# A ring of six value pages where the spread queries lay: paged attention in a two-layer decoder step

## The reference, cut to what matters

```python
def fox_sample(q, k, v, logf, k_pool, v_pool, lf_pool, page_table):
    k_past = k_pool[page_table].reshape(bd, p_len, h, d)
    v_past = v_pool[page_table].reshape(bd, p_len, h, d)
    ...
    s_past = (jnp.einsum('bqhd,bkhd->bhqk', q, k_past).astype(jnp.float32) * scale
              + cq[..., :, None] + jnp.transpose(r_past, (0, 2, 1))[:, :, None, :])
    ...
    p = jax.nn.softmax(jnp.concatenate([s_past, s_new], axis=-1), axis=-1)
    return (jnp.einsum('bhqk,bkhd->bqhd', p[..., :p_len].astype(v.dtype), v_past)
            + jnp.einsum('bhqk,bkhd->bqhd', p[..., p_len:].astype(v.dtype), v))
```

## Time and profile before

| | |
|---|---|
| median of 3 runs | 2034.9 us (2031.11 to 2038.15) |
| the profiled execution | 2039.11 us, span 2037.5 us |
| TensorE busy, weight loads busy | 87%, 75% of the span |
| VectorE, ScalarE, GpSimd busy | 47%, 27%, 5% |
| DMA over the span | 110 GB/s; in the loop over slots 230 to 270 GB/s |
| mean granted TensorE clock | 0.925 |

### The profile page before, as it was taken

The page is one execution under the profiler, slowest core; times in us unless marked ns, Lnnn a source line. Parts: engine busy times, 40 slices in busy tenths (PEclk is TensorE's granted clock), DMA queues, the critical chain, the costliest instruction groups (busy, mean ns, idle before and its releaser), DMA issues.

```text
span 2037.5 us, 37876 instructions
## 1 busy us (share of the span) xinstructions
PE 1767.3 (87%) x15111; PEld 1537.3 (75%) x15111; DVE 948.9 (47%) x1377; ACT 556.1 (27%) x992; POOL 105.1 (5%) x208
## 2 busy tenths in 40 slices
PE   5999555989999999799966787777779899999998
PEld 4876433979999999799944444444439799999997
DVE  5388776453333322467455755555513533333222
ACT  3210223232222211243331333333312322222110
POOL 1000000000000000144410000000000000000000
PEclk9999876999999999999977788888879899999999
DMA  3211031222222323222341677777662122223221
GB/s 117 61 43 32 24 96 42 83 62 81 80 81 80 95 72 85 66 71 76 102 164 58 218 260 256 262 264 271 239 197 77 55 82 82 82 82 98 72 85 60
DMA packets 239470, 224.79 MB, mean 110 GB/s; under 512 B 12114, under 2 KB 199588, under 8 KB 239354
## 3 DMA queue, kind: packets, MB, share of 16 engines
q1 hardware_dynamic: 229168, 200.83, 31.7%
q0 software_dynamic: 8768, 19.09, 2.9%
q10 hardware_dynamic: 1418, 3.29, 0.5%
HBM read 215.37 MB, written 7.80 MB: 110 GB/s over the span
## 4 chain that ended last, share of the span: by engine, by line
PE 74%; DVE 12%; DMA 5%; issue 3%; ACT 3%; SPq 3%; ACTq 0%; DVEq 0%; POOL 0%; POOLq 0%
PE ps L1484 56%; DMA vring<-in_cache_fox_v_dram 4%; PE ps L1897 4%; PE ps L1673 3%; PE ps L1942 2%; PE ps L1466 1%; DVE tmp L438 1%; SPq L2060 1%; PE ps L1876 1%; DVE yc L717 1%; DVE aL L442 1%; DVE rb L448 1%; DVE rb L433 1%; PE ps L1535 1%; PE ps L1858 1%
## 5 line engine op out<-in xcount | busy, mean ns | idle before, releaser
L1484 PE MATMUL ps<-aH,wH 128*128 128x288 f32 x2224 | 488.3, 301 | 49.8 <-DVE aL L442 34.2
L1484 PE MATMUL ps<-aL,wH 128*128 128x288 f32 x2224 | 480.7, 298 | 0.0
L1484 PE MATMUL ps<-aH,wL 128*128 128x288 f32 x2224 | 480.4, 298 | 0.0
L1484 PEld LDWEIGHTS ps<-aH,wH 128*128 128x128 f32 x2224 | 362.2, 191 | 59.3 <-issue 35.6
L419 DVE TENSOR_TENSOR wL<-raw,wH 128x1024 fp32r<-128x1024 f32 (+1 forms) x179 | 232.0, 1296 | 338.4 <-ACT wH L1053 335.3
L1484 PEld LDWEIGHTS ps<-aL,wH 128*128 128x128 f32 x2224 | 363.1, 191 | 0.0
L1484 PEld LDWEIGHTS ps<-aH,wL 128*128 128x128 f32 x2224 | 362.5, 191 | 0.0
L1053 ACT ACTIVATE wH<-raw 128x1024 fp32r<-128x1024 f32 (+1 forms) x179 | 199.0, 1112 | 388.0 <-PE ps L1484 359.4
L1484 PE MATMUL ps<-gH,wH 128*128 128x288 f32 x704 | 151.8, 297 | 4.8 <-DVE gL L635 4.8
L1484 PE MATMUL ps<-gL,wH 128*128 128x288 f32 x704 | 151.5, 296 | 0.0
L1484 PE MATMUL ps<-gH,wL 128*128 128x288 f32 x704 | 151.5, 296 | 0.0
(11 more groups left out here) (306 smaller groups left out, 1788.3 us busy)
## 6 DMA issues: line engine op xcount, KB each, us to landing
kset<-in_cache_fox_k_dram SPq DMA_DIRECT2D x128, 384.0 KB, 4.2
vring<-in_cache_fox_v_dram SPq DMA_DIRECT2D x128, 384.0 KB, 4.8
raw<-in_w_gate_up_dram SPq DMA_DIRECT2D x88, 512.0 KB, 3.7
raw<-in_w_down_dram SPq DMA_DIRECT2D x32, 704.0 KB, 4.6
raw<-in_fox_w_in_dram SPq DMA_DIRECT2D x21, 512.0 KB, 4.0
raw<-in_w_out_dram SPq DMA_DIRECT2D x16, 512.0 KB, 3.9
raw<-in_conv_w_in_dram SPq DMA_DIRECT2D x14, 512.0 KB, 3.9
raw<-in_w_mem_kv_dram SPq DMA_DIRECT2D x8, 512.0 KB, 3.7
```

Of the source, the lines that this page charges most:

```text
L1484: mm = nc.tensor.matmul(ps[:, 2 * slot + h, 0:HT], weights[:, w], a[:, k0 + k, h * HT:(h + 1) * HT], start=(first and k == 0 and weights i ...
```

## The change

The value ring gets six buffers in place of four. The two new ones take the bytes of `qr`, which is removed with its 16 copies, its semaphore and ACT's two waits ahead of them. `spread` instead copies each sequence's queries straight from `qkT` into `qx4`, with 16 instructions of 32 partitions x 48 elements where there were four of 128 x 48. The SP queue keeps its order of keys and values; at each place where a value page was issued, the page two further on is issued, and it waits for the same page to be used as before (page n now waits for page n-6, not n-4). Six pages, not four, are issued ahead of the turns. SP's loop gets one more turn, in which nothing is issued. TensorE's and VectorE's instructions stay as they are.

```diff
-    VRING = 4
+    VRING = 6
...
-        qr, o = at("qr", [P, NH, 2, NS], o)
...
-            act.wait_ge(hn_done, Z + 1 + HP)
-            act.wait_ge(mL_done, KD)
-            for e in range(2):
-                for c in range(2):
-                    r = slice(DH * e + DQ * c, DH * e + DQ * c + DQ)
-                    for a in range(4):
-                        last = nc.scalar.activation(qr[DQ * a:DQ * a + DQ].rearrange("p (g e) c n -> p g e c n", e=2)[:, :, e, c, :],
-                                                    qkT[r, 0:HP, SEQ:T], ACT.Copy)
-            last.then_inc(qr_done, 1)
...
-                for m in range(4):
-                    nc.scalar.activation(qx4[:].rearrange("p (j m c) n -> p j m c n", m=4, c=2)[:, :, m, :, NQ * m:NQ * m + NQ],
-                                         qr[:].rearrange("p (j m) c n -> p j m c n", m=4)[:, :, m, :, NQ * b:NQ * b + NQ], ACT.Copy)
+                for e in range(2):
+                    for c in range(2):
+                        for a in range(4):
+                            rows = slice(DH * e + DQ * c, DH * e + DQ * c + DQ)
+                            mine = qx4[DQ * a:DQ * a + DQ, 2 * e + c, NQ * e:NQ * e + NQ]
+                            mine = bass.AP(tensor=mine.tensor, offset=mine.offset, ap=[mine.ap[0], [8 * QR, 3], [4 * QR + 2 * NQ, 2], [1, NQ]])
+                            nc.scalar.activation(mine, qkT[rows, 0:HP, SEQ + NQ * b:SEQ + NQ * b + NQ].rearrange("p (j m) q -> p j m q", m=2), ACT.Copy)
...
-            for s in range(SLOTS + SPB - 1):
+            for s in range(SLOTS + SPB):
...
-                for n in range(4 * (s - 3), 4 * (s - 2)):
-                    if n >= VRING:
+                for n in range(4 * (s - 4) + VRING, 4 * (s - 3) + VRING):
+                    if VRING <= n < NB * NP:
                         value_page(n)
```

More of the change, by code:

```diff
@@ L352, in build @@
         e_done, zab_done, c_ready, c_done, stage_done = (sem(n) for n in ("e_done", "zab_done", "c_ready", "c_done", "stage_done"))
-        lftot_done, qr_done, clear_done = (sem(n) for n in ("lftot_done", "qr_done", "clear_done"))
+        lftot_done, clear_done = (sem(n) for n in ("lftot_done", "clear_done"))
         turn_ready = sem("turn_ready")
```

## The result

The change made the kernel slower by 0.4%: 2046.16 us as a median of 9 runs (2042.56 to 2053.17), beside 2037.78 us (2030.58 to 2041.2) for the kernel before on the same chip; ratio 1.0044, 95% interval 1.003 to 1.0059. The profiled execution took 2050.02 us, span 2048.4; the mean granted clock of TensorE went from 0.925 to 0.917. The forecast was 2005 us, faster.

The account below looks back on a forecast made before the run. Weight products, untouched, were 56% of the span's chain; in the slot loop, value-page landings held TensorE. Odd slots 35 plus drain 9.5 less spread 15 made 30 us less: 2005 us on the median, range 1991 to 2026.

Parts of the forecast that it names:

- The ring's mechanism: Twelve odd slots, 5 to 27: the batch's first landing gates the third page, no longer the first; wait 46.9 to about 20.
- The first landing: T0, when an odd slot's first value page issued behind the keys lands, some 9 us behind the set; taken to stay.
- The burst's 4 us: Page bursts follow each other without rest, so landings come later: 0 to 13 us over twelve slots, 4 taken as cost.
- the fetch: TensorE's 2.27 us stop in second sets, read as code fetch behind page traffic, grows: 0 to 22 us, 6 taken.
- The ring's sum: Odd slots gain 45.4 us, less 4 for the burst and 6 for code fetch: 35 us; the drain adds 9.5.
- The working of slot 13: Slot 13: values ahead of the landing run at their shorter durations, so the next set begins 3.96 us earlier.
- The drain: From slot 28 on, values alone: the last sixteen pages' issues take 16.7 us instead of 26.06, 9.5 us less.
- The spread: ACT's query copies ahead of first sets: twelve more cost 1.9 us a spread, 15 us over eight (12 to 23).
- `qr`: Its sixteen building copies on ACT, 0.52 us each, end; 7.9 us of slack there, so nothing gained.
- The slower one: Rival: moving between quadrants sets the copy's price, 7.8 us more a spread, 62 in all: 2052 us; chance 0.08.
- The copies that do not overlap: Rival: short spread copies at 0.34 us each, 39 us more in all: 2029 us, about no change; chance 0.05.
- The wait that only moves: Rival: TensorE can't run the step's values ahead of the landing, a slot gains some 1.5 us: 2026 to 2039; chance 0.07.

Follow-up runs that it names:

- the ring alone: The changed kernel with six value buffers but the spread as four wide copies without the quadrant shift (wrong queries): 2011.69 us, ratio 0.989 to the kernel before.
- the spread alone: The changed kernel with its sixteen narrow spread copies and no `qr`, but four value buffers in the old load order: 2072.48 us, ratio 1.0181 to the kernel before.
- the moved reduction: The changed kernel with the sample's first reduction on VectorE moved from the fourth slot's head to the third's end: 2037.52 us, ratio 1.0016 to the kernel before.
- the run without the shift between quadrants: The changed kernel with its sixteen spread copies reading the same quadrant that they write (wrong queries): 2041.08 us.
- the queue's run on the kernel before: The kernel before with SP's queue alternating two key pages and two value pages in each turn, nothing else: 2048.88 us, ratio 1.0079.
- the queue interleaved: The changed kernel with spread copies on GpSimd, early sample reduction, and SP's queue alternating two key and two value pages: 1998.77 us, ratio 0.9817 to the kernel before.

## Why the prediction was wrong

- **The ring's mechanism: right.** The wait stands at the third page, 1.42 us in the row above, and ahead of the drain it is 17.7 us in all (24.2 less 6.5), where about 20 were forecast. The first landing stays where it was: 8.2 us behind the keys' first issue (1231.62 to 1239.84), 9.1 before. The burst's 4 us did not come, nor did the fetch: the time called issue ahead of the sets was 13.2 us with the ring alone, 12.9 before.
- **The ring's sum: the step that failed.** The working of slot 13 let the values run at their shorter durations once the stall was gone, 1.06 and 1.09 for 2.18 and 1.97, and left every other line at the duration that it had. With the ring alone the values did get that (26.3 us less), and the other lines took 32 us more: the half clock was not removed, it moved (granted to the sets' products: 0.92 before, 0.76 with the ring alone). Forecast 44.5 us with the drain, measured 20.
- **The drain: right.** From the last set's values to the last product of the attention: 37.9 us before (1482.99 to 1520.88), 29.4 after (1502.57 to 1531.95); 8.5 less for 9.5.
- **The spread: mis-sized, a second step that failed.** Twelve more copies cost 2.8 us a spread at 0.237 each, said the upper bound, and 1.9 was taken. The rows show 4.00 + 0.68 us for 1.20, 3.5 more, which is above the bound too, since the first four lost their overlap as well. TensorE's idle time ahead of the sets grew by 22.2 us, where the sum had 15, and with the spread alone by 26.0; the time lost by the spread alone was 37. The step took the overlap of copies of 64 and 128 partitions, most of them on the same partitions as the copy before, for one that copies of 32 from quadrant to quadrant have as well. One of its own rows spoke against that: the sixteen starts of line 1321 lie some 0.53 us apart at 0.52 us each. And the 0.15 of the qx copies is a mean over steps of some 0.11 and 0.13 us within a half and one of 0.22 across. The misses at the ring and at the spread, 24 and 22 us, are alike in size. The Trainium skill's budget (ScalarE: Activation LUTs, "Rules for kernel authors") is given there for a bias that is a pointer operand, which these copies do not pass; its estimate of 0.34 us a copy for 48 elements lies as far above the 0.25 of these rows as the 0.16 that was taken lies below.
- **VectorE's list: missed.** No step asked what comes next in the fourth slot once the pages no longer do: 10.7 us more of waits ahead of the sample's transposes, of which the moved reduction took 5.1 off that wait (14.0 to 8.9) and perhaps 6 us off the time.
- **`qr`: not seen.** No row of after speaks against the nothing forecast for its removal; no run tried it alone.
- **The rivals.** The slower one had the right sign and the wrong cause: the run without the shift between quadrants has copies of the same length, and a copy takes 0.25 us, under its 0.38. It put the end on the other side by the spread alone, and that alone would not have done it: 44.5 less 37 is still a gain. The copies that do not overlap, given a chance of 0.05, are what came, at 0.25 and not 0.34 us each; by the forecast's other terms that alone would have left a gain (35 + 9.5 - 28 = 16 us). The wait that only moves named TensorE's long durations, but on the step's values ahead of the third page, and there they went away. No rival had the half clock move to the sets.

What stays open is why the sets, and not the lines ahead of them, get most of the half clock with the ring of six, why shorter waits cost clock in the queue's run on the kernel before, and whether a copy's change of partitions or its width of 32 takes the overlap. Of the spread alone the profiled execution has 23.9 us as waits and 12.0 as longer products.

## What to carry to other kernels

A wait that is removed from a bound engine is worth what the engine does next: price it with the granted clock of the work behind it, and ask on which products the half clock will lie afterwards. Where a wait only gets shorter, and moves from ahead of cheap work to ahead of dear work, it can cost more than it did, as the queue's run on the kernel before has it. And write down, for every engine that writes its list in order, when it would be through if the work ahead came 4 us earlier; here that was VectorE, late with the ring of six (14.0 us of waits for 3.3) and late again with the queue interleaved (14.9 for 7.0).

## What was not expected of the hardware

On ScalarE sixteen copies of 32 x 48 elements took 4.00 us, four of 128 x 48 took 0.63. Two copies of 64 x 24 on the same half of the partitions started 0.13 us apart, and 0.22 apart when the second was on the other half. GpSimd did the sixteen in 4.41 us, each waiting for the one before. And TensorE did 21.3 us more work at no cost of time when that work lay in its pauses, because waits shrank and, in the executions compared, other products got 17.3 us shorter.
